# Shifted bias table, four-tile state products, later top-k steps and a last row by halves in a two-layer streaming encoder step

## The chip, the cores and the metric

The kernel runs on one core of a Trainium2 chip, written by hand for each engine: TensorE (PE, with its weight loads PEld), VectorE (DVE), ScalarE (ACT), GpSimd (POOL) and SyncE (SP), which issues most of the DMAs. The metric is the device time of one execution in microseconds (us). Three runs of the kernel before took 1894.93, 1895.78 and 1898.64 us; their median, 1895.78 us, is the time before.

## The reference

One inference step of a two-layer hybrid encoder over 640 tokens: 512 frames of a new stream (prompt) and 8 running streams of 16 frames (sample). All is fp32.

```python
def rmsnorm(x, g):
    xf = x.astype(jnp.float32)
    y = xf * lax.rsqrt(jnp.mean(xf * xf, axis=-1, keepdims=True) + EPS)
    return (y * g.astype(jnp.float32)).astype(x.dtype)
...
# layer 0, per query: score all visible keys with a small indexer, keep the top ones, attend to them
score = jnp.einsum('bqhs,bqh->bqs', jax.nn.relu(s), wi_b.astype(jnp.float32)) * IDX_SCALE
score = jnp.where(visible[None], score, -jnp.inf)
top_s, top_i = lax.top_k(score, top)
bias = bias_tab[rel_bucket(top_i - pos_b[None, :, None])]
logits = (jnp.einsum('bqgjd,bqkgd->bqgjk', q_b, k_sel).astype(jnp.float32) * ATTN_SCALE
          + jnp.moveaxis(bias, 2, -1))
probs = jax.nn.softmax(logits, axis=-1).astype(v_sel.dtype)
...
# layer 1: a Mamba-2 mixer: in-projection, causal conv of 4 taps, SiLU, chunked state recurrence
def step(s, inp):
    st, dec = inp
    return s * dec[..., None, None] + st, s
...
x = x + out.astype(x.dtype)
x = x + sqrelu_mlp(rmsnorm(x, norm_ffn[i]), mlp_w_up[i], mlp_w_down[i]).astype(x.dtype)
```

The outputs are the normalized x of both groups, and the new keys, values, indexer keys, conv rows and states. There are 16 heads of 64 with 4 key/value heads, 8 SSM groups of 4 heads, d_model 1024, d_ff 4096. The top of a query is 128 keys of 512 (prompt) or 132 of 528 (sample).

## The kernel before, in words

**Layout.** Activations lie transposed in SBUF: `xT` is 128 partitions x 8 chunks x 640 tokens. Every large product is split in three (high x high, low x high, high x low parts of fp32): for each of 8 chunks of the contraction, three weights by two halves of 320 tokens (`chunk_products`, line 206), so 48 matmuls a block of 128 output columns. A block's weights are loaded by SP into one of two slots (`load_slab`, L181), split by ACT (`split_hi`, L194: `WH`) and DVE (`split_lo`, L198: `WL`), and its product stands in two PSUM banks: 0 and 1, or 2 and 3, by the block's parity. A slot's load waits until the weights two blocks before have been split.

**What orders the work.** There is no scheduler: every engine has a program written out in order, and waits on semaphores. An instruction that waits holds up all that stands behind it on its engine.

**Stages, with their place in the time of the profile.**
1. 0 to 119 us: x is turned, block by block the indexer queries, indexer keys, keys and values are projected. The relative-position table (32 buckets x 16 heads) is expanded by a product with a one-hot matrix (L2328), copied by ACT (`tb_stage`), stored to DRAM (L2119) and read back skewed, 16 rows at a time, into `biasP` and `biasS` (L2127, L2137) by the same SP queue that loads the weights. The norm's scales are spread over the partitions by `norm_pe_spread` (L287).
2. 119 to 187 us: eight query blocks; between the halves of each, the cached indexer keys and the sample scores; DVE runs the 16 top-k rounds of the prompt.
3. 187 to 286 us: prompt attention in 64 units (2 key/value pairs x 4 query tiles x 8 heads; tile t has 128(t+1) keys). POOL adds mask and bias into `BM` (L2247 for the far keys, which share one bias `cfar`; L2249 for the near ones), PE multiplies (L2423), DVE adds and takes the maximum (`maxed`, L2964), ACT takes the exponent (L2697), PE turns (L2436) and weighs (L2450). Once in 8 units `spread_sums` (L2462) spreads the inverse sums, 8 products of 64 columns into bank 7, which ACT copies (L2714) before the next exponent. Between the units DVE makes the masks (`mask_step`) and runs the sample's top-k (`sample_top`: L2951, L2953, L2955), one step a unit.
4. 286 to 347 us: sample attention. 347 to 405 us: the attention's output blocks `B_O` to `B_O + 7`, added to x (L426).
5. 405 to 839 us: the MLP of layer 0, as pairs of 128 columns, with products by quarters (L1370, L1398). The rows of the last pairs are added to x by `add_row` (L1616).
6. 839 to 1446 us: the SSM. Eight groups of six blocks; during group g the products of group g-1 (u) finish. Within a group's first two blocks PE turns the old sample states (`pe_turn_prev`, L554, into banks 6 and 7), ACT copies them (`copy_prev`, L912), PE makes the states' new parts (`pe_sample_states`, L565, banks 4 and 5) and DVE adds them (`sample_states`, L719, 8 instructions). POOL multiplies the decays (`multiply_w`, L1047). The last group finishes beside the output blocks `B_OUT`.
7. 1446 to 1893 us: the MLP of layer 1 and the final norm: sums (L1811), the last chunk's squares (L1820), turned rows (L1799), scaled by ACT (L1839) and DVE (L1855), stored by SP (L1916).

## Time and profile before

| what | value |
|---|---|
| median of three runs | 1895.78 us |
| the profiled execution, its own time | 1895.32 us |
| its span | 1893.4 us |
| mean granted TensorE clock | 0.993 |
| PE, DVE, ACT, POOL busy | 98%, 67%, 42%, 16% |
| chain that ended last: PE | 86% |
| the same: DVE, issue, ACT, DMA | 4%, 4%, 3%, 1% |

The execution's own time is 1.9 us more than its span. The span runs from the first instruction to the last; what lies around it is start and the landing of the last stores. A busy share of PE is not PE at its peak, since the ends of matmuls are modelled. The chain is followed back from the last instruction, and the shares tell on which engine the time passed.

### The profile page before, as it was taken

How to read it: one execution, taken by the hardware profiler on the slowest of the kernel's cores; microseconds unless marked ns; L12 is line 12 of the kernel's file. 1: busy time of each engine (PE TensorE's matmuls, PEld its weight loads, DVE VectorE, ACT ScalarE, POOL GpSimd, SP SyncE). 2: the span in 40 equal slices, each digit the busy share in tenths (PEclk: the TensorE clock that was granted, in tenths of full speed). 3: DMA queues.
4: the chain of work that ended last, by engine and by line, in shares of the span. 5: the costliest groups of instructions: out<-in, count | busy, mean ns of one | idle time of the engine just before them, and what ended most of it. 6: DMA issues, size and time to landing. Idle time of an engine off the chain costs nothing.

```text
span 1893.4 us, 35381 instructions
## 1 busy us (share of the span) xinstructions
PE 1848.0 (98%) x13223; PEld 1737.0 (92%) x13223; DVE 1271.5 (67%) x2357; ACT 801.7 (42%) x1435; POOL 303.5 (16%) x356
## 2 busy tenths in 40 slices
PE   8899899999999999999999999999999999999998
PEld 7777566899999999999999999999899999999998
DVE  4388875447758586447787888888554775858653
ACT  4232674334334343334465544656333434434332
POOL 0001651110000000022333343332112000000001
PEclk9999999999999999999999999999999999999999
DMA  6732203331322223322433444335423132222321
GB/s 154 128 74 53 64 24 125 77 95 57 112 62 73 84 78 94 97 55 82 129 101 123 130 133 133 102 122 164 148 67 110 51 112 62 83 75 87 92 68 56
DMA packets 311571, 176.88 MB, mean 93 GB/s; under 512 B 39888, under 2 KB 305040, under 8 KB 310416
## 3 DMA queue, kind: packets, MB, share of 16 engines
q1 hardware_dynamic: 308752, 172.49, 32.3%
q10 hardware_dynamic: 2688, 2.62, 0.5%
q8 instruction: 86, 1.41, 0.3%
q14 instruction: 45, 0.37, 0.1%
HBM read 155.18 MB, written 19.72 MB: 92 GB/s over the span
## 4 chain that ended last, share of the span: by engine, by line
PE 86%; DVE 4%; issue 4%; ACT 3%; DMA 1%; SPq 1%; DVEq 0%; POOL 0%; ACTq 0%
PE psum L206 29%; PE psum L1370 28%; PE psum L1398 14%; PE psum L589 1%; PE psum L2423 1%; PE psum L2436 1%; PE psum L2515 1%; PE psum L2450 1%; PE psum L565 1%; DMA W<-attn_w_in 1%; PE psum L593 1%; PE psum L554 1%; PE psum L542 1%; DVE conv_out L708 1%; PE psum L2354 1%
## 5 line engine op out<-in xcount | busy, mean ns | idle before, releaser
L206 PE MATMUL psum<-b2H,WH 128*128 128x320 f32 x912 | 218.2, 321 | 1.2 <-DVE xT L1616 0.9
L206 PE MATMUL psum<-b2H,WL 128*128 128x320 f32 x912 | 208.6, 310 | 0.0
L206 PE MATMUL psum<-b2L,WH 128*128 128x320 f32 x912 | 208.4, 310 | 0.0
L1370 PE MATMUL psum<-b2H,HT 128*128 128x320 f32 x816 | 186.2, 309 | 1.1 <-DVE xT L426 1.1
L1370 PE MATMUL psum<-b2L,HT 128*128 128x320 f32 x816 | 186.0, 309 | 0.0
L194 ACT ACTIVATE WH<-W 128x1024 fp32r<-128x1024 f32 x90 | 95.0, 1055 | 201.9 <-PE psum L206 161.5
L198 DVE TENSOR_TENSOR WL<-W,WH 128x1024 fp32r<-128x1024 f32 x90 | 139.7, 1552 | 55.8 <-ACT WH L194 54.9
L1398 PE MATMUL psum<-HH,HT 128*128 128x320 f32 x544 | 167.4, 308 | 1.5 <-DVE HL L1487 1.5
L1398 PE MATMUL psum<-HL,HT 128*128 128x320 f32 x544 | 167.8, 308 | 0.0
L206 PEld LDWEIGHTS psum<-b2H,WH 128*128 128x128 f32 x912 | 150.0, 190 | 16.0 <-issue 12.6
L206 PEld LDWEIGHTS psum<-b2L,WH 128*128 128x128 f32 x912 | 153.4, 189 | 0.0
L1370 PE MATMUL psum<-b2H,LT 128*128 128x320 f32 x672 | 153.1, 309 | 0.0
L206 PEld LDWEIGHTS psum<-b2H,WL 128*128 128x128 f32 x912 | 153.1, 189 | 0.0
L1426 DVE SCALAR_TENSOR_TENSOR HF<-psum,RS 128x640 f32<-128x640 f32 (+1 forms) x70 | 53.1, 766 | 136.6 <-PE psum L1370 129.3
L1398 PE MATMUL psum<-HH,LT 128*128 128x320 f32 x448 | 138.0, 308 | 0.0
L1370 PEld LDWEIGHTS psum<-b2H,HT 128*128 128x128 f32 x816 | 136.3, 188 | 1.4 <-issue 1.4
L248 POOL COPY ACC<-SQ 128x640 f32<-128x640 f32 x4 | 4.3, 1072 | 825.8 <-ACT SQ L235 786.1
L1370 PEld LDWEIGHTS psum<-b2L,HT 128*128 128x128 f32 x816 | 136.3, 188 | 0.0
L206 PE MATMUL psum<-b1H,WH 128*128 128x320 f32 (+1 forms) x528 | 125.9, 320 | 6.6 <-DVE WL L198 5.2
L1431 ACT ACTIVATE HF<-HF 128x640 f32<-128x640 f32 (+1 forms) x70 | 48.4, 692 | 190.2 <-DVE HF L1426 190.2
L206 PE MATMUL psum<-b1H,WL 128*128 128x320 f32 (+1 forms) x528 | 121.6, 312 | 0.0
L206 PE MATMUL psum<-b1L,WH 128*128 128x320 f32 (+1 forms) x528 | 121.2, 311 | 0.0
(398 smaller groups left out, 4368.1 us busy)
## 6 DMA issues: line engine op xcount, KB each, us to landing
W<-ssm_w_in SPq DMA_DIRECT2D x98, 256.0 KB, 3.1
RW<-mlp_w_up SPq DMA_DIRECT2D x64, 256.0 KB, 3.0
RWx<-mlp_w_up SPq DMA_DIRECT2D x64, 256.0 KB, 3.0
RW<-mlp_w_down SPq DMA_DIRECT2D x64, 256.0 KB, 3.1
RWx<-mlp_w_down SPq DMA_DIRECT2D x64, 256.0 KB, 3.1
bc<-scratch_acs SPq DMA_DIRECT2D x8, 1280.0 KB, 7.5
W<-attn_w_in SPq DMA_DIRECT2D x32, 256.0 KB, 3.9
prev<-state_ssm SPq DMA_DIRECT2D x16, 512.0 KB, 5.3
```

The lines of the kernel that those rows point to most:

```text
L194: act.activation(WH[:, b.slot], W[:, b.slot], ACT.Copy).then_inc(w_hi, 1)
L198: dve.tensor_tensor(WL[:, b.slot], W[:, b.slot], WH[:, b.slot].bitcast(F32), ALU.subtract).then_inc(w_lo, 1)
L206: last = pe.matmul(psum[0:m, 2 * b.slot + h, 0:TH], w[:, b.slot, k, 0:m], r[:, k, h * TH:(h + 1) * TH], start=(n == 0 and i == 0), stop=(n ...
L542: last = pe.matmul(bank(4, 1024, 2)[:, 256 * t + P * p:256 * t + P * p + P], Btok[:, t * P:(t + 1) * P], xddt[:, p, t * P:(t + 1) * P], st ...
L554: last = pe.transpose(bank(6, 1024, 2)[:, b * P:(b + 1) * P], prev[:, p, b], ident)
L565: last = pe.matmul(bank(4 + k), xddt[r, p, SEQ:T], Bx[r, 4 * k:4 * k + 4].rearrange("p b n -> p (b n)"), start=True, stop=True)
L589: pe.matmul(bank(6, T, 2)[64 * h:64 * h + 64, t * P:(t + 1) * P], xdt[:, p, t * P + 64 * h:t * P + 64 * h + 64], Wm[:, 2 * p + h, t * P:(t ...
L593: pe.matmul(psum[:, 4, (t - 1) * P:t * P], ST[:, t - 1, p * P:(p + 1) * P], C2[:, t * P:(t + 1) * P], start=True, stop=True)
L1370: last = pe.matmul(psum[:, i // 2 * 2 + h, 0:TH], w[:, k], x, start=(kx == 0 and c == 0), stop=(kx == 7 and c == 2))
L1398: last = pe.matmul(down_bank(g, i), w[:, k], x[:, DNB[i], k], start=(k == 0 and c == 0), stop=(k == 3 and c == 2))
L1426: dve.scalar_tensor_tensor(t, src, 0.0, rs, ALU.max, ALU.mult).then_inc(h_rl, 1)
L1431: act.activation(t, t, ACT.Square).then_inc(h_sq, 1)
```

## The change

- **Table.** The one-hot row of the far bucket gets -1 everywhere, so that every bias is taken relative to the far one (softmax does not see a shift common to a head). `cfar` and its load go. POOL's far part becomes a copy of the mask, and only for the first four units after a change of tile.
- **Bias loads.** The 16 loads of `biasP` and `biasS` move from between the blocks 4, 5 and 6 into the first six query blocks on SP. The table's product and the turned vectors come ahead of `norm_pe_spread` and of two products of block 1 on PE.
- **Attention.** `sample_top` starts at unit 18 in place of 12, the sample's mask at 52 in place of 46. `spread_sums` alternates between the two halves of the columns.
- **Banks at two stage changes.** Block `B_O + 7` goes to banks 6 and 7, row 1 of pair 31 to banks 4 and 5, and the first products of the next stage wait for one block or row less.
- **SSM.** `pe_sample_states` is 4 products of 32 rows x 256 columns into banks 4 to 7, in place of 2 of 64 x 512 into 4 and 5; it now waits for `copy_prev` too. DVE's `sample_states` of the first half comes ahead of `split_lo`. ACT's SiLU of the second gate (`silu_second`) moves from a group's end to behind the first `copy_prev` of the next, and the second `copy_prev` comes ahead of `silu_rows`.
- **End.** The last row is multiplied, added and squared by halves of the tokens; the sums come between the halves. The last tile is scaled half by ACT and half by DVE, and its store is issued by ACT.

```diff
@@ shape_constants
+    onehot[half - 1] -= 1.0
@@ Block
+            self.out = 6 if c == B_O + 7 else 2 * self.slot
@@ pe_turn_prev, p == 1
+            pe.wait_ge(fss, 16 * u + 4)
@@ pe_sample_states
         pe.wait_ge(bxs, u + 1)
+        pe.wait_ge(pvc, 3 * u + p + 1)
...
-        for k in range(2):
-            r = slice(64 * k, 64 * k + 64)
-            last = pe.matmul(bank(4 + k), xddt[r, p, SEQ:T], Bx[r, 4 * k:4 * k + 4].rearrange("p b n -> p (b n)"),
+        for i in range(4):
+            r = slice(32 * i, 32 * i + 32)
+            last = pe.matmul(psum[:, 4 + i, 0:256], xddt[r, p, SEQ:T], Bx[r, 2 * i:2 * i + 2].rearrange("p b n -> p (b n)"),
                              start=True, stop=True)
@@ sample_states
-        for b in range(DB):
+        for b in (4, 5, 6, 7, 0, 1, 2, 3):
@@ ssm_group_dve
-        conv_evac(dve, g, 0)
+        conv_evac(dve, g, 0, (lambda: sample_states(dve, u, 0)) if L else None)
...
-        if L:
-            sample_states(dve, u, 0)
         conv_taps(dve, g, 0)
@@ ssm_group_act
+    def silu_second(act, u):
+        act.wait_ge(out_free, (Block(B_SSM + 5, 3 * u)).n + 1)
+        act.activation(sz[:, 1], sz[:, 1], ACT.Silu).then_inc(zs, 1)
...
         split_hi(act, b0(0), 4)
+        if L:
+            silu_second(act, u)
+            copy_prev(act, u, 1)
...
         silu_rows(act, g, 0)
-        if L:
-            copy_prev(act, u, 1)
...
-        act.wait_ge(out_free, (Block(B_SSM + 5, 3 * g)).n + 1)
-        act.activation(sz[:, 1], sz[:, 1], ACT.Silu).then_inc(zs, 1)
@@ rows_pe
+    def row_bank(g, r):
+        return 4 if (g, r) == (31, 1) else 2 * r
...
-                    pe.wait_ge(out_free, last_block(layer, i // 2) + 1)
+                    pe.wait_ge(out_free, B_O + 6 if (g, i) == (0, 0) else last_block(layer, i // 2) + 1)
...
+                last_row_pe(pe)
+                return
...
+    def last_row_pe(pe):
...
+        for h in range(2):
+            for i in (2, 3):
+                n, b = n0 + i, ((0, 3), (4, 5))[i % 2][h]
+                for k in range(4):
+                    for c, (w, x) in enumerate(((HT[h_tile(n)], HH), (HT[h_tile(n)], HL), (LT[l_tile(n)], HH))):
+                        last = pe.matmul(psum[:, 2 + h, 0:TH], w[:, k], x[:, b, k],
+                                         start=(i == 2 and k == 0 and c == 0), stop=(i == 3 and k == 3 and c == 2))
+            last.then_inc(sw_mm, 1)
+            if h == 0:
+                final_sums(pe)
@@ mlp_dve, the last row of layer 1
+            for h in range(2):
+                dve.wait_ge(sw_mm, op0(63) + 3 + h)
+                dve.wait_ge(sw_cb, 56)
+                dve.tensor_tensor(x_half(7, h), psum[:, 2 + h, 0:TH], x_half(7, h), ALU.add).then_inc(sw_rx, 1)
@@ final_pe
-        pe.wait_ge(sq_ready, 40)
-        for t in range(NT):
-            last = pe.matmul(psum[:, 0, t:t + 1], SQ[:, 1, t * P:(t + 1) * P], ones[:], start=False, stop=(t == NT - 1))
-        last.then_inc(x_turn, 1)
+        pe.wait_ge(sw_rx, 17)
+        final_squares(pe, 1).then_inc(x_turn, 1)
@@ tail_pe
-        pe.wait_ge(sw_rx, 8)
+        pe.wait_ge(sw_rx, 6)
         multiply(pe, Block(B_DT), b2H, b2L, ready=(gx_lo, 16), order=ORD)
@@ tail_dve, last group
         add_to_x(dve, Block(B_OUT), 0)
+        sample_states(dve, u, 0)
         split_lo(dve, Block(B_OUT + 2))
-        sample_states(dve, u, 0)
         add_to_x(dve, Block(B_OUT + 1), 1)
+        sample_states(dve, u, 1)
         split_lo(dve, Block(B_OUT + 3))
-        sample_states(dve, u, 1)
@@ sync, query blocks
+                if b < 6:
+                    for n in range((0, 2, 4, 7, 10, 13)[b], (2, 4, 7, 10, 13, 16)[b]):
+                        load_bias_p(DS * n) if n < 8 else load_bias_s(n - 8)
@@ gpsimd, units
-                if far:
-                    pool.tensor_tensor(BM[:, u % 4, 0:far], maskP[:, OFF[t]:OFF[t] + far],
-                                       cfar[:, h:h + 1].broadcast_to([P, far]), ALU.add)
+                if far and u % 8 < 4 and TILES[u // 8 - 1][1] != t:
+                    pool.tensor_copy(BM[:, u % 4, 0:far], maskP[:, OFF[t]:OFF[t] + far])
@@ tensor, first blocks
             first_products(1, 4)
+            first_products(0, 7)
+            pe.wait_ge(c_in, 112)
             pe.wait_ge(x_ready, 8)
-            norm_pe_spread(pe, 0)
-            first_products(0, 7)
-            first_products(1, 5)
-            pe.wait_ge(c_in, 112)
             pe.matmul(psum[0:NH, 7, 0:512], rb_stage[:], oh_stage[:, 0:512], start=True, stop=True)
...
+            norm_pe_spread(pe, 0)
+            first_products(1, 5)
@@ spread_sums
-                for gj in range(8):
-                    gp, j = gj // 4, gj % 4
-                    last = pe.matmul(psum[64 * gp:64 * gp + 64, 7, j * P:(j + 1) * P],
-                                     rinv[:, w % 2, 2 * j + gp:2 * j + gp + 1].broadcast_to([P, 64]), ident, start=True, stop=True)
+                for j in range(4):
+                    for gp in range(2):
...
@@ vector, units
-                if 12 <= u < 46:
-                    sample_top(u - 12)
-                if 46 <= u < 53:
+                if 18 <= u < 52:
+                    sample_top(u - 18)
+                if 52 <= u < 59:
```

**SP, from the table's constants to the first query blocks.** `W` is the weight slot of `load_slab`, `scratch_bias` the table in DRAM. Before:

```order
L181 DMA W<-attn_w_in 128x4x128 x2
L2119 DMA scratch_bias<-tb_stage 256x1x656
L181 DMA W<-attn_w_in 128x4x72 x2
L2127 DMA biasP<-scratch_bias 16x16x256 x4
L181 DMA W<-attn_w_in 128x4x128 x2
L2127 DMA biasP<-scratch_bias 16x16x256 x4
L181 DMA W<-attn_w_in 128x4x128 x2
L2137 DMA biasS<-scratch_bias 16x2x528 x8
L2140 DMA cfar<-rel_bias 128x16
L181 DMA W<-attn_w_in 128x4x128 x4
L2145 DMA kiT<-kiT 64x640
L2146 DMA scratch_wi<-wiT 8x128
```

With the change:

```order
L183 DMA W<-attn_w_in 128x4x72 x2
L2173 DMA scratch_bias<-tb_stage 256x1x656
L183 DMA W<-attn_w_in 128x4x128 x6
L2178 DMA kiT<-kiT 64x640
L2179 DMA scratch_wi<-wiT 8x128
L183 DMA W<-attn_w_in 128x4x128 x2
L2184 DMA wcol<-scratch_wi 16x8x1 x8
L2203 DMA KI<-cache_idx_k 128x4x64 x4
L183 DMA W<-attn_w_in 128x8x64 x8
L2203 DMA KI<-cache_idx_k 128x4x64 x2
L2191 DMA biasP<-scratch_bias 16x16x256 x2
L183 DMA W<-attn_w_in 128x8x64 x2
```

The loads of `biasP` no longer stand between those of `W`; the first two come behind `KI` and eight loads of `W`, in the first query block.

**ACT, from the last group's exponent on.** `Wm` is the decays, `prevT` the turned sample states, `sz` the gate. Before:

```order
L957 ACTIVATE Wm<-Wm 128x2560
L1012 ACT_TABLE_LOAD
L1012 ACTIVATE sz<-sz 128x640
L912 ACTIVATE prevT<-psum 128x8x128
L194 ACTIVATE WH<-W 128x1024
L912 ACTIVATE prevT<-psum 128x8x128
```

With the change:

```order
L959 ACTIVATE Wm<-Wm 128x2560
L914 ACTIVATE prevT<-psum 128x8x128
L196 ACTIVATE WH<-W 128x1024
L963 ACT_TABLE_LOAD
L963 ACTIVATE sz<-sz 128x640
L914 ACTIVATE prevT<-psum 128x8x128
```

The gate's table load and SiLU have gone from between the exponent and the first copy of `prevT` to behind the first split.

**DVE, in a group's first block.** `raw` is the block taken from PSUM, `prev` the sample states, `WL` the low part of the next weights. Before:

```order
L689 TENSOR_TENSOR raw<-psum,RS 128x192
L690 TENSOR_TENSOR raw<-psum,RS 128x8x16
L198 TENSOR_TENSOR WL<-W,WH 128x1024
L719 SCALAR_TENSOR_TENSOR prev<-prev,EXp,psum 128x128 x8
L711 TENSOR_SCALAR conv_out<-raw,cw 128x664
L708 SCALAR_TENSOR_TENSOR conv_out<-raw,cw,conv_out 128x664 x3
```

With the change:

```order
L692 TENSOR_TENSOR raw<-psum,RS 128x192
L693 TENSOR_TENSOR raw<-psum,RS 128x8x16
L722 SCALAR_TENSOR_TENSOR prev<-prev,EXp,psum 128x128 x8
L200 TENSOR_TENSOR WL<-W,WH 128x1024
L714 TENSOR_SCALAR conv_out<-raw,cw 128x664
L711 SCALAR_TENSOR_TENSOR conv_out<-raw,cw,conv_out 128x664 x3
```

The eight steps on `prev` have moved ahead of the split of the next weights.

## Rows read from the trace of the kernel before

**Rows 1.** page, busy time, share of the span and instructions of each engine

```profile
PE 1848.0 (98%) x13223; PEld 1737.0 (92%) x13223; DVE 1271.5 (67%) x2357; ACT 801.7 (42%) x1435; POOL 303.5 (16%) x356
```

**Rows 2.** chain that ended last, 25 to 125 us; start, length, what

```profile
54.29 13.97 DMA W<-attn_w_in
```

**Rows 3.** who waited for whom, whole run; total us, times, longest us

```profile
PE psum L206 <- DVE WL L198: 5.2, 2, 4.6
...
PE psum L1370 <- DVE xT L426: 1.1, 1, 1.1
...
PE psum L206 <- DVE xT L1616: 0.9, 1, 0.9
...
PE psum L565 <- DVE prev L719: 1.0, 1, 1.0
```

**Rows 4.** busy time by stretch; PE, PEld, DVE, ACT, POOL, then PE clock, DMA share, GB/s

```profile
60.00:66.00 6.00, 5.58 (x22) 5.58 (x23) 1.92 (x3) 0.00 (x0) 0.00 (x0) 0.54 1.19 176
66.00:70.00 4.00, 4.00 (x28) 3.73 (x26) 0.62 (x1) 1.06 (x1) 0.00 (x0) 1.00 1.05 208
206.20:216.60 10.40, 8.24 (x72) 5.04 (x73) 9.99 (x28) 4.85 (x16) 7.88 (x12) 1.00 0.46 136
276.10:284.00 7.90, 6.82 (x66) 4.68 (x66) 3.70 (x20) 5.63 (x25) 3.24 (x10) 1.00 0.42 138
```

**Rows 5.** timeline of VectorE and TensorE, 27 to 29 us

```profile
27.57 0.88 DVE L239 SCALAR_TENSOR_TENSOR b1L<-xT,vcol,b1H 128x640 fp32r<-128x640 f32 x1
27.80 1.35 PE L287 MATMUL psum<-cst,rs 128*128 128x128 f32 x10 [1.01 <-DVE rs L282]
```

**Rows 6.** DMA issues, 0 to 130 us; KB each, median us to landing

```profile
W<-attn_w_in SPq DMA_DIRECT2D x28, 256.0 KB, 4.3
...
biasP<-scratch_bias SPq DMA_DIRECT2D x8, 256.0 KB, 11.7
```

**Rows 7.** timeline of the SP queue, 105 to 350 us

```profile
137.02 1.00 SPq L181 DMA_DIRECT2D W<-attn_w_in  x2
```

**Rows 8.** chain that ended last, 120 to 187 us

```profile
165.59 3.71 PE psum L206 x24
```

**Rows 9.** chain that ended last, 187 to 292 us

```profile
228.51 1.18 PE psum L2462 x13
229.97 0.07 PE psum L2462
...
234.31 1.02 PE psum L2450 x16
...
288.86 0.86 PE psum L2515 x2
```

**Rows 10.** chain that ended last, 1136 to 1196 us

```profile
1148.52 1.06 PE psum L565 x4
...
1162.46 1.00 PE psum L576 x16
```

**Rows 11.** timelines of ACT, DVE and POOL, 1143 to 1154.2 us

```profile
1144.06 2.34 ACT L957 ACTIVATE Wm<-Wm 128x2560 f32<-128x2560 f32 x1
...
1148.76 0.49 DVE L688 TENSOR_TENSOR raw<-psum,RS 128x320 f32<-128x320 f32 x1 [2.18 <-PE psum L206]
...
1150.35 3.08 DVE L198 TENSOR_TENSOR WL<-W,WH 128x1024 fp32r<-128x1024 f32 x1 [0.64 <-ACT WH L194]
...
1146.64 5.71 POOL L1047 TENSOR_TENSOR Wm<-Wm,cbm 128x2560 f32<-128x2560 f32 x1 [14.24 <-ACT Wm L957]
```

**Rows 12.** timelines of ACT and PE, 1325 to 1338 us

```profile
1325.82 2.34 ACT L957 ACTIVATE Wm<-Wm 128x2560 f32<-128x2560 f32 x1
...
1327.06 1.13 PE L565 MATMUL psum<-Bx,xddt 64*128 64x512 f32 x4 [0.47 <-DVE ST L799]
```

**Rows 13.** chain that ended last, 1860 us to the end

```profile
1879.65 1.01 PE psum L1811 x10
...
1881.38 1.25 PE psum L1820 x10
```

More of the change, by code:

```diff
@@ L205, in chunk_products @@
             for h in range(2):
-                last = pe.matmul(psum[0:m, 2 * b.slot + h, 0:TH], w[:, b.slot, k, 0:m],
+                last = pe.matmul(psum[0:m, b.out + h, 0:TH], w[:, b.slot, k, 0:m],
                                  r[:, k, h * TH:(h + 1) * TH],
@@ L425, in add_to_x @@
         xd = xT[:, d] if isinstance(d, int) else xT[:, bass.ds(d, 1)].rearrange("p o t -> p (o t)")
-        dve.tensor_tensor(halves(xd), out_all(b.slot), halves(xd), ALU.add).then_inc(out_free, 1)
+        dve.tensor_tensor(halves(xd), psum[:, b.out:b.out + 2, 0:TH], halves(xd), ALU.add).then_inc(out_free, 1)
     s2 = [S0]
@@ L1764, in mlp_act @@
                 down_act(act, g, end)
-        next_act(act, layer, 7)
+        if layer:
+            act.wait_ge(acc_done, 38)
+            for h in range(2):
+                act.wait_ge(sw_rx, 16 + h)
+                act.activation(SQ[:, 1, h * TH:(h + 1) * TH], x_half(7, h), ACT.Square).then_inc(sq_ready, 1)
+        else:
+            next_act(act, layer, 7)
         if layer == 0:
@@ L1781, in mlp_dve @@
                 down_dve(dve, g, end)
-        add_row(dve, 32 * layer + 31, 1)
+        if layer:
+            for h in range(2):
+                dve.wait_ge(sw_mm, op0(63) + 3 + h)
+                dve.wait_ge(sw_cb, 56)
+                dve.tensor_tensor(x_half(7, h), psum[:, 2 + h, 0:TH], x_half(7, h), ALU.add).then_inc(sw_rx, 1)
+            dve.wait_ge(sw_rx, 17)
+        else:
+            add_row(dve, 31, 1)
         next_dve(dve, layer, 7)
@@ L1811, in final_pe, with final_squares @@
             pe.matmul(psum[:, 0, t:t + 1], ACC[:, t * P:(t + 1) * P], ones[:], start=(t == 0), stop=False)
+    def final_squares(pe, half):
+        pe.wait_ge(sq_ready, 40 + half)
+        for t in ((0, 1), (2, 3, 4))[half]:
+            last = pe.matmul(psum[:, 0, t:t + 1], SQ[:, 1, t * P:(t + 1) * P], ones[:], start=False, stop=(t == NT - 1))
+        return last
+    def final_pe(pe):
+        final_squares(pe, 0)
         pe.wait_ge(newton, 16 + 7)
@@ L1814, in final_pe @@
             y_turn(pe, t, ORD[6])
-        pe.wait_ge(sw_rx, 16)
-        for i in range(4):
+        pe.wait_ge(sw_rx, 17)
+        final_squares(pe, 1).then_inc(x_turn, 1)
+        for i in range(KC - 1):
             y_turn(pe, 2, ORD[i])
-        pe.wait_ge(sq_ready, 40)
-        for t in range(NT):
-            last = pe.matmul(psum[:, 0, t:t + 1], SQ[:, 1, t * P:(t + 1) * P], ones[:], start=False, stop=(t == NT - 1))
-        last.then_inc(x_turn, 1)
         for i in range(4, KC - 1):
@@ L1913, in tail_sp @@
             load_pair(sp, g)
-        for t in range(NT):
+        for t in range(4):
             sp.wait_ge((rs_ready, newton)[t % 2], (8 + 2, 16 + 14)[t % 2] + t // 2)
-            sp.dma_start(O["y_prompt"].rearrange("b s d -> (b s) d")[P * t:P * t + P, :] if t < 4 else
-                         O["y_sample"].rearrange("b i d -> (b i) d"), y_tok[:, t]).then_inc(store, 16)
+            sp.dma_start(O["y_prompt"].rearrange("b s d -> (b s) d")[P * t:P * t + P, :], y_tok[:, t]).then_inc(store, 16)
         for s, n in ((pv_st[0], SG), (pv_st[1], SG), (sp_st, SG), (y_st, SG - 1), (store, 8 + NT)):
@@ L2152, in _, with load_bias_p, load_bias_s @@
                                  allow_slow_non_contiguous=True).then_inc(wi_col, 16)
+            bt = S["bias"]
+            def load_bias_p(p0):
+                sp.dma_start(biasP[p0:p0 + DS], skew(bt, -REL0 - P - p0, [[NREL - 1, DS], [DS * NREL, NH], [1, 256]])
+                             ).then_inc(bias_in, 16)
+            def load_bias_s(gj):
+                sp.dma_start(biasS[DS * gj:DS * gj + DS],
+                             skew(bt, gj * DS * NREL + DS - 1,
+                                  [[NREL - 1, DS], [8 * DS * NREL, 2], [1, KEYS_S]])).then_inc(bias_in, 16)
             def load_ki(b):
@@ L2459, in spread_sums @@
                 wait(pe, rbc, w)
-                for gj in range(8):
-                    gp, j = gj // 4, gj % 4
-                    last = pe.matmul(psum[64 * gp:64 * gp + 64, 7, j * P:(j + 1) * P],
-                                     rinv[:, w % 2, 2 * j + gp:2 * j + gp + 1].broadcast_to([P, 64]), ident, start=True, stop=True)
+                for j in range(4):
+                    for gp in range(2):
+                        last = pe.matmul(psum[64 * gp:64 * gp + 64, 7, j * P:(j + 1) * P],
+                                         rinv[:, w % 2, 2 * j + gp:2 * j + gp + 1].broadcast_to([P, 64]), ident,
+                                         start=True, stop=True)
                 last.then_inc(rsp, 1)
@@ L2635, in _ @@
             act.sem_inc(sq_ready, 3)
+            split_hi(act, Block(2))
             norm_act_copy(act, 0)
-            for b in range(2, 9):
+            act.wait_ge(v_rdy, 4)
+            act.activation(tb_stage[:, 0:512], psum[0:NH, 7, 0:512], ACT.Copy)
+            act.activation(tb_stage[:, 512:NREL], psum[0:NH, 4, 256:256 + NREL - 512], ACT.Copy).then_inc(v_rdy, 1)
+            for b in range(3, 9):
                 split_hi(act, Block(b))
-                if b == 2:
-                    act.wait_ge(v_rdy, 4)
-                    act.activation(tb_stage[:, 0:512], psum[0:NH, 7, 0:512], ACT.Copy)
-                    act.activation(tb_stage[:, 512:NREL], psum[0:NH, 4, 256:256 + NREL - 512], ACT.Copy).then_inc(v_rdy, 1)
             def index_relu(n):
```

64 lines of the change are left out of this document (33 added, 31 removed).

## The prediction

> **What bounds the kernel.** I read the busy times first. TensorE is busy 98% of the span [rows 1], VectorE 67%, ScalarE 42%, GpSimd 16%. A change can therefore shorten the time in two ways only: it removes a wait of TensorE, or it removes work of TensorE. Work saved on the others counts only where TensorE waits for them. The span is 1893.4 us; the profiled execution's own time is 1895.32 us, which lies 0.46 us under the median of the runs. The sum is made on the former, and 0.46 is added at the end.
>
> Next I read who waited for whom on TensorE, which gives four waits that the diff touches [rows 3]: 5.2 us in two for the low weights `WL` (the longest 4.6 us), 1.1 and 0.9 us at the two stage changes, 1.0 us for the sample states of the last group. Then I read the stretches around them: clock and load [rows 4], the chain of the attention [rows 9], of an SSM group [rows 10] and of the end [rows 13].
>
> **Start, 0 to 119 us.** The reader sees in the chain that a DMA of `W` took 13.97 us from 54.29 on [rows 2], where such a load of 256 KB takes 4.3 us in the middle case [rows 6]. The loads of `biasP`, of which each has the same 256 KB and a median of 11.7 us [rows 6], stood ahead of it in the same queue. This slab's split came too late, and TensorE stood still for 4.6 us. With the change no bias load stands between these slabs, so both waits go: -5.2 us. The standing still had a second price. From 60 to 66 us TensorE had a granted clock of 0.54, its lower level of 1.2 GHz, and 22 matmuls took 5.58 us; right behind, at a clock of 1.00 (2.4 GHz), 28 took 4.00, 0.143 each [rows 4]. At that pace the 22 take 3.14, so -2.4 us more.
>
> Against it: the one-hot product now comes ahead of the norm's spread product and takes a place among the first products, and the spread's successor waits for the low parts of x. VectorE finishes the last of these at 27.57 + 0.88 = 28.45 [rows 5]. TensorE waited 1.01 us until 27.80 before, so it was free at 26.79, and now it stands until 28.45, 1.66 us: +0.65. The one-hot constants must be there earlier; I take 0, with an upper end of +0.5. Start in all: -5.2 - 2.4 + 0.65 = -6.95.
>
> **Query blocks, 119 to 187 us.** The bias loads now stand here, two or three a block, on the same SP queue. A slab issued at 137.02 [rows 7] belongs to the products that TensorE begins at 165.59 [rows 8], 28 us later, about 26 after the splits. Even a landing of 13.97, as seen behind such loads, leaves 12 us. So I price the move at 0; without this lead it would cost what it cost at the start. The attention's first biases are wanted only after 187 us.
>
> **Attention, 187 to 286 us.** `spread_sums` stands in the chain with 13 records and 1.18 us at 228.51 and its last at 229.97, to 230.04: 1.53 us from first to last [rows 9]. ScalarE must copy the result before its next exponent. The turned products of L2450, which go by pairs of column halves, put 16 records into 1.02 us [rows 9], one per 0.064. L2462 before ran all four of one half of the columns and then all four of the other. Alternating halves should bring it to about 1.02, 0.5 less, of which I take 0.45. It happens 8 times, in 7 of them with the exponents waiting behind: -3.2. Bounds: 0, if the two halves do not lie beside each other, and -4.
>
> The top-k of the samples goes six steps later. From 206.2 to 216.6 us VectorE is busy 9.99 of 10.40 us and TensorE 8.24; from 276.1 to 284, where six steps now land, VectorE is busy 3.70 of 7.90 [rows 4]. The six steps of about 0.6 us are taken out of the full stretch, and about a third of that reaches TensorE: -1.3, between -2.3 (the whole of TensorE's 2.16 idle there) and +0.5 (they delay the last units' maxima). The masks then come six units later, and the loads behind them still land before the sample products at 288.86. GpSimd's lighter `BM` I count at 0: it was 7.88 of 10.40 busy in the full stretch, not the last to arrive. Attention: -4.5.
>
> **Stage changes.** The waits of 1.1 and 0.9 us [rows 3] are for the last block or row to leave its banks. With spare banks they go; with the refill 0.1 more: -2.1. The next that could be late is the last chunk of x, wanted only behind seven other chunks, which is hidden.
>
> **SSM.** Two products of 64 rows x 512 columns are 4 records in 1.06 us [rows 10]. One product of this kind with 512 columns, L2515, is 2 records in 0.86 [rows 9]. So the two lie beside each other, with some 0.2 fixed, else they would take 1.72. Four of 32 rows x 256 columns side by side would take 0.43 + 0.2 = 0.63, a gain of 0.43. Bounds, for 32-row tiles no row shows: best 0.43 (-0.63); pairwise only, 1.06 (0); one after the other 1.92 (+0.86). I take side by side, since 16 records of L576, tiles by columns, fit into 1.00 [rows 10], and price 7 groups x 2 x -0.43 = -6.0.
>
> The Trainium skill, "TensorE: Matmul & The Clock Gate", Part 3 on packing small matmuls, gives four 32-row tiles of 512 columns a measured speedup of 3.07. By it 1.72 would become about 0.56, an estimate, and the gain would be 0.50 in place of 0.43, -7.0 in all. No run here shows it yet.
>
> The product now waits for ScalarE's copy of the old states too. In a steady group the exponent ends at 1144.06 + 2.34 = 1146.40 [rows 11]; the copy behind it takes about 1.0, so to 1147.4, and TensorE wants it at 1148.52 [rows 10]: 1.1 us to spare, 0. Queued behind a late copy would be all of TensorE. The second turn now waits for four of VectorE's steps on the states. They stand ahead of the split, behind the copies of `raw`, about 1149.7 to 1150.8, and are wanted some 2 us later: 0. This holds if these steps are not slowed beside GpSimd's product of the decays, which runs from 1146.64 for 5.71 [rows 11]. Beside it `raw`, with one input from SBUF and one from PSUM, took 0.49, while the split, both inputs in SBUF, took 3.08 [rows 11]. The steps on `prev` take PSUM and SBUF, so I count them undisturbed.
>
> The Trainium skill, "SBUF — State Buffer", on who interferes with whom, says the same of a VectorE instruction with two SBUF inputs against a reading GpSimd one, and that whichever starts first blocks the other. By this the split, which now starts about 1 us later, would wait less; the sum does not change, since its result is wanted far later.
>
> In the last group ScalarE has its exponent until 1325.82 + 2.34 = 1328.16 [rows 12]; before, TensorE began its product at 1327.06, since it didn't wait for the copy. Now it can start at 1328.16 + 1.01 = 1329.17 at the earliest: +2.1. Then the later wait of 1.0 for the states [rows 3] goes and two products are cheaper by 0.86: +0.2 net.
>
> **End.** The sums L1811 (1.01) and squares L1820 (1.25) stand behind the last row [rows 13]. The sums now run between the halves, and two of five squares are done early, against smaller instructions on the way: -0.4. The stores behind are bound by the transfers, so who issues them moves nothing. Bounds -1.5 and +0.5.
>
> **Sum.** -6.95 - 4.5 - 2.1 - 6.0 + 0.2 - 0.4 = -19.75. 1895.32 - 19.75 = 1875.6, and with 0.46: 1876.
>
> **Rivals.**
> - *32-row tiles do not lie beside each other four at a time.* For it: no row has them. Against: the 64-row ones do. The 14 products gain nothing: 1876 + 6 = 1882. In full series they cost 14 x 0.86 in place of -6.0, +18: 1894, no change.
> - *Another half-clock spell.* The last group's wait of 2.6 us (0.47 + 2.1) or the 1.66 us of the start could bring what the 4.6 us brought. Price 2.4 to 3.5 us: 1879.5. Against: the rows show one only behind 4.6 us.
> - *The attention passes the wait on.* ScalarE's exponents wait on VectorE's maxima, so shorter spreading is given back: 0 in place of -4.5, 1880.5.
> - *The states' steps are blocked beside GpSimd* as the split is (3.08 against about 1.2): then the second turn comes about 0.7 late in 7 groups: +4.9, 1881.
> - *The slower one: the bias loads starve the query blocks.* Here the queue has 16 more loads within 60 us. It decides once a slab lands more than 26 us after its issue, against 13.97 seen. If slabs came 5 us late in five of the blocks, 25 us would come on top: 1901. Against: the share of the DMA engines is under half in most stretches of the middle part (0.46, 0.42), though over 1 at 60 to 70 us [rows 4].
>
> **How the numbers follow.** 0.66 for the forecast (its own range 1871 to 1881, from the bounds of the top-k, spreading and tile terms), 0.12 for tiles without a gain, of which 0.02 is full series; 0.10 for a new spell, 0.05 for the attention, 0.04 for blocked steps, 0.03 for starved query blocks. The range goes from 1869, where tiles, spreading and the end all reach their lower ends (-2.8, -0.8, -1.1 and -1.0 from the top-k, -5.7 together, and 1 for small waits), to 1885. About 0.2%, 3.8 us, is what a measurement can tell from no change: faster, under 1892, has all but the starved blocks and full series: 0.95; same 0.02; slower 0.03.
>
> **What would show it.** Start: TensorE without a wait for `WL` over 1 us and a granted clock of 1.00 from 60 to 66 us; if a wait stays, the term falls. Query blocks: no wait for `WL` from 119 to 187. Attention: L2462's successor with 16 records in about 1.0. SSM: four tiles with starts within 0.1 and about 0.63 in all; a wait for `prevT` in steady groups would be against me. Last group: TensorE waits about 2.6 us for `prevT` and none for `prev`. I am wrong outside the range if the tiles run serially or a slab of the query blocks comes late.

## The result, and the profile after

| | us |
|---|---|
| before, median of 4 runs | 1895.36 |
| changed, median of 4 runs (1876.36 to 1880.72) | 1878.08 |
| ratio, 95% interval | 0.9909, [0.9893, 0.9925] |
| profiled execution: own time, span | 1876.36, 1874.6 |

The change makes the kernel 17.3 us faster by the medians, 19.0 us by the two profiled executions (1895.32 against 1876.36). Forecast was 1876, range 1869 to 1885. The busy times after, as those of [rows 1]:

```profile
PE 1834.3 (98%) x13290; PEld 1731.4 (92%) x13290; DVE 1259.0 (67%) x2359; ACT 802.1 (43%) x1436; POOL 290.1 (15%) x336
```

The last store lands 0.48 us ahead of the span's end in both executions (1892.97 and 1874.09), so what an execution takes beyond its span, 1.8 to 1.9 us, is not that landing.

TensorE is still the bound. Its work is 13.7 us less. Since both kernels issue almost the same products in the same order, the best view of where the time went is the start of the same product in both traces. Each number is the growth, over one stage, of the start after minus the start before. A clock stretch is a time in which TensorE's granted clock was 0.50, its lower level of 1.2 GHz:

| stage | forecast | measured | of which |
|---|---|---|---|
| start and query blocks, to the first L2501 (193.29 before, 188.24 after) | -6.95 | -5.05 | the two waits for `WL` are gone, a clock stretch has moved to 29 to 36 us |
| attention, to 288.15 / 275.65 | -4.5 | -7.45 | -2.7 is a clock stretch (193 to 199 us) that did not come |
| two stage changes, to 846.71 / 831.69 | -2.1 | -2.5 | |
| begin of the SSM, to 898.14 / 883.85 | 0 | +0.7 | -3.05 and +3.8, below |
| seven SSM groups, to 1280.83 / 1259.53 | -6.0 | -7.0 | |
| last group, to 1342.04 / 1322.51 | +0.2 | +1.8 | a clock stretch behind the wait |
| end, to TensorE's last (1886.24 / 1866.87) | -0.4 | +0.2 | |
| stores behind it | 0 | +0.5 | from the first issue to the last landing 8.34 us, before 7.86 |

The waits of TensorE, whole run, that answer to [rows 3] (columns: who waited for whom, total us, times, longest):

```profile
PE psum L208 <- DVE b1L L241: 2.6, 3, 1.8
PE psum L568 <- ACT prevT L914: 2.6, 1, 2.6
PE psum L536 <- ACT Btok L998: 2.0, 1, 2.0
```

All four waits of [rows 3] are gone. Three others stand there. The first and the second were forecast (1.66 and 2.6 us; they are 1.8 and 2.56); the third, 2.0 us for `Btok`, was not. The stretches around them, as in [rows 4] (PE, PEld, DVE, ACT, POOL, then PE clock, DMA share, GB/s):

```profile
28.00:36.00 8.00, 7.81 (x28) 5.38 (x29) 1.99 (x6) 2.08 (x4) 0.00 (x0) 0.58 0.18 37
50.00:60.00 10.00, 10.00 (x71) 9.75 (x69) 2.73 (x3) 1.69 (x2) 0.00 (x0) 1.00 0.27 74
191.00:199.00 8.00, 6.31 (x61) 3.85 (x59) 6.80 (x25) 5.41 (x19) 5.96 (x9) 1.00 0.47 159
871.00:878.00 7.00, 5.18 (x38) 4.91 (x36) 6.78 (x8) 1.57 (x5) 4.12 (x7) 1.00 0.48 156
878.00:884.00 6.00, 5.78 (x31) 5.81 (x32) 4.26 (x3) 5.89 (x8) 4.09 (x4) 0.72 0.15 38
...
191.00:199.00 8.00, 7.04 (x35) 4.37 (x33) 4.92 (x19) 3.86 (x17) 3.28 (x5) 0.57 0.13 37
871.00:878.00 7.00, 7.00 (x28) 6.70 (x28) 4.44 (x5) 5.16 (x8) 0.35 (x2) 0.51 0.34 92
878.00:884.00 6.00, 6.00 (x43) 6.00 (x42) 5.12 (x9) 1.06 (x1) 1.33 (x2) 1.00 0.65 176
```

The first five rows are of the changed kernel, the last three of the one before. From 50 to 60 us, where the kernel before stood still for 4.6 us, TensorE is now busy all the time at 1.00. But from 28 to 36 us it had a granted clock of 0.58, where it ran 28 matmuls in 7.81 us. The stretch at 0.50 of the kernel before at 191 to 199 us is absent (1.00), and the one at 871 to 878 has its counterpart at 878 to 884 (0.72). Inside the kernel these stretches last 3.41 or 6.83 us in all fourteen profiles. At half the clock a TensorE that is busy throughout does 1.7 or 3.4 us less work in them; where it also waits in them, the starts of equal products show somewhat less (1.5, 2.7 us).

The products of the states and the spread sums, as in [rows 9] and [rows 10] (chain that ended last):

```profile
218.70 1.05 PE psum L2513 x16
...
1130.20 0.64 PE psum L568 x8
...
1138.94 0.64 PE psum L568 x8
```

`spread_sums` has 16 records in 1.05, 0.48 less than before; the four row tiles take 0.64, forecast 0.63, where the two took 1.06.

The last group, as in [rows 11] and [rows 12] (timelines of ACT and PE):

```profile
1304.52 2.34 ACT L959 ACTIVATE Wm<-Wm 128x2560 f32<-128x2560 f32 x1
1306.77 1.00 ACT L914 ACTIVATE prevT<-psum 128x1024 f32<-128x1024 f32 x1
...
1307.87 0.71 PE L568 MATMUL psum<-Bx,xddt 32*128 32x256 f32 x8 [2.56 <-ACT prevT L914]
...
1309.66 0.73 PE L208 MATMUL psum<-b2H,WH 128*128 128x320 f32 x2
1310.19 0.73 PE L208 MATMUL psum<-b2L,WH 128*128 128x320 f32 x2
```

The exponent ends at 1306.86, the copy at 1307.77, and L568 starts 0.10 later behind 2.56 us of standing still. That is as forecast. The pairs of matmuls right behind it take 0.53 from start to start (1309.66 to 1310.19) in place of 0.29: the lower clock. It costs 1.5 us more, which was only among the rivals.

### The profile page after: what moved, and what is told of

It reads as the page before. It is cut to its first block, busy times and chain, and to the rows that moved or that the text cites. A ratio compares the mean times of both kernels' runs of the same rounds, so it can differ in the third digit from the quotient of the medians.

```text
span 1874.6 us, 35518 instructions
## 1 busy us (share of the span) xinstructions
PE 1834.3 (98%) x13290; PEld 1731.4 (92%) x13290; DVE 1259.0 (67%) x2359; ACT 802.1 (43%) x1436; POOL 290.1 (15%) x336
## 4 chain that ended last, share of the span: by engine, by line
PE 88%; DVE 4%; issue 3%; ACT 3%; DMA 0%; DVEq 0%; POOL 0%; SPq 0%; ACTq 0%
PE psum L208 32%; PE psum L1380 27%; PE psum L1426 14%; PE psum L592 1%; PE psum L2474 1%; PE psum L2567 1%; PE psum L2487 1%; PE psum L556 1%; PE psum L596 1%; PE psum L2501 1%; PE psum L543 1%; PE psum L2405 1%; PE psum L568 1%; PE psum L2591 1%; DVE conv_out L711 0%
## 5 line engine op out<-in xcount | busy, mean ns | idle before, releaser
L200 DVE TENSOR_TENSOR WL<-W,WH 128x1024 fp32r<-128x1024 f32 x90 | 126.7, 1408 | 27.2 <-ACT WH L196 27.0
```

The lines of the kernel that those rows point to most:

```text
L200: dve.tensor_tensor(WL[:, b.slot], W[:, b.slot], WH[:, b.slot].bitcast(F32), ALU.subtract).then_inc(w_lo, 1)
```

## The experiments

Each kernel was compared with the changed one by the starts of equal products in the profiles. "Theory" and "rival" below are what was expected before each run. Medians have 4 or 5 runs (the very last one a single run). The runs of one kernel differ by up to about 7 us, in part by clock stretches that fall here or there, so effects of 1 to 4 us are read from the traces.

**The state products again as two of 64 rows.**

```diff
-        for i in range(4):
-            r = slice(32 * i, 32 * i + 32)
-            last = pe.matmul(psum[:, 4 + i, 0:256], xddt[r, p, SEQ:T], Bx[r, 2 * i:2 * i + 2]...
+        for k in range(2):
+            r = slice(64 * k, 64 * k + 64)
+            last = pe.matmul(bank(4 + k), xddt[r, p, SEQ:T], Bx[r, 4 * k:4 * k + 4]...
...
```

VectorE's `sample_states` reads banks 4 and 5 accordingly.

> The changed kernel, but the new parts of the sample states again as 2 products of 64 rows x 512 columns in place of 4 of 32 x 256; waits and orders stay as changed. Theory (four row tiles lie beside each other, and this is the whole gain of the SSM stage): L568 goes from 0.65 us a time to about 1.06, and the stage gets 0.41 x 16 = 6.6 us longer, about 1884.5 in all. Rival (the stage's gain comes from the moved waits and the order on ScalarE and VectorE, not from the product): the product's time is hidden by a wait behind it, and the stage stays within 1.5 us of the changed kernel's.

Measured: 1882.83 us, ratio to before 0.9935 [0.9916, 0.9954]. In the chain of its trace:

```profile
1132.86 1.06 PE psum L568 x4
...
1142.03 1.06 PE psum L568 x4
```

1.06 each, and each of the 14 in the steady groups moves all that follows by 0.39 to 0.42 us: +5.5 at the last group. The product is the gain of the SSM stage; the rival falls. In all its last product of TensorE is 4.3 us later: the last group loses less, since its clock stretch at 1309 us did not come (-1.5).

**`spread_sums` by one half of the columns and then the other.**

```diff
-                for j in range(4):
-                    for gp in range(2):
+                for gp in range(2):
+                    for j in range(4):
```

> The changed kernel, but spread_sums writes all four products of the one column half and then all four of the other. Theory: the 16 records take about 1.5 us in place of 1.0, and each of the seven times that exponents wait behind costs 0.48: +3.4 us in the attention, about 1881. Rival (the wait is passed on): the records take longer but the stage's length changes by under 1 us.

Measured: 1880.44 us. The chain has it as the kernel before:

```profile
218.15 1.18 PE psum L2513 x13
```

ScalarE's copies behind it come later by 0.47 to 0.48 us each of eight times: from 1.02 us ahead of the changed kernel at the first to 2.30 behind at the last, with 1.49 ahead of all. So 3.8 us, and nothing is passed on. Forecast was 0.45 seven times; it is 0.48 eight times, none is hidden. The profiled execution is only 2.0 us longer than the changed kernel's, since its stretch at 31 us was the short one (1.5 us less); its other stretches nearly cancel.

**Top-k from unit 12 again.**

```diff
-                if 18 <= u < 52:
-                    sample_top(u - 18)
+                if 12 <= u < 46:
+                    sample_top(u - 12)
```

and the sample's mask from unit 46.

> The changed kernel, but the samples' top-k starts at unit 12 and their mask at unit 46 again. Theory: the 1.7 us that TensorE gained in units 12 to 17 go again, and nothing is gained at the end: +1.7 us, about 1879.7. Rival (the gain there came from GpSimd's lighter bias or from elsewhere): 0. Also watched: whether the stretch at half the clock at the attention's begin, which one profile of the kernel before showed (191.8 to 198.6 us) and that of the changed one did not, appears; all instructions up to there are those of the changed kernel, so that a difference would be chance.

Measured: 1880.61 us. The waits of TensorE, 195 to 215 us, of this kernel and then of the changed one:

```profile
PE psum L2513 <- DVE rinv L3022: 1.5, 1, 1.5
...
PE psum L2513 <- DVE rinv L3022: 0.2, 1, 0.2
```

The third call of `spread_sums` waits 1.5 us for VectorE's inverse sums, 0.2 with the later top-k (the kernel before had this wait too, 1.53 us at 215.04): the start of its first product is 1.43 us later, and no difference arises from there to the end of the attention but a clock stretch at 207 to 211 us (0.56). Forecast -1.3, measured -1.4, but the place is one wait, not a third of the load taken off VectorE: that the sizes meet is luck. At the attention's begin no stretch at half the clock came. In five of the fourteen profiles of this case it did (before, bias loads back, table first, sums behind both halves, the four mends once), in the others not.

**Bias loads between the slabs again.**

```diff
-            for b in range(5, 8):
-                load_slab(sp, Block(b), slab_g1(b))
+            for p0 in range(0, 64, DS):
+                load_bias_p(p0)
+            load_slab(sp, Block(5), slab_g1(5))
...
```

The other loads follow between blocks 6 and 7, and those in the query blocks go.

> The changed kernel, but the 16 bias loads stand between the weight slabs of blocks 4 to 7 on SP again. Theory: TensorE waits some 5 us for WL near 55 to 62 us and then runs at the lower clock level for 3 to 7 us: +7 to +8 us, about 1885. Rival A (the 4.6 us wait came from the table's store and read-back, which both stand early here too, so the slabs are late only as far as TensorE is early): +3 to 5. Rival B (the loads cost nothing here since the spell at half the clock at 29 to 36 us has slowed TensorE by then): under 2.

Measured: 1886.77 us, ratio 0.9952 [0.9935, 0.997]. Waits of TensorE 60 to 130 us, and its stretches:

```profile
PE psum L208 <- DVE WL L200: 4.4, 2, 3.6
...
62.00:69.00 7.00, 4.91 (x34) 4.65 (x32) 0.00 (x0) 0.88 (x1) 0.00 (x0) 1.00 1.17 180
69.00:75.00 6.00, 4.51 (x22) 4.51 (x23) 2.40 (x3) 1.24 (x2) 0.30 (x1) 0.72 1.03 216
```

The wait is 4.4 us in all, followed by a clock of 0.72 from 69 to 75 us. From 0.50 us ahead of the changed kernel at 58 us it goes to 5.74 behind at the first L2396 (79.03), 6.2 us: 4.5 of waiting and refill and 1.7 of clock. That lies between the theory (7 to 8) and rival A; rival B falls. The rest of the 9.9 us in this profile are clock stretches at 192 to 200 and 281 to 286 us.

**Table ahead of the last first product.**

```diff
             first_products(1, 4)
-            first_products(0, 7)
             pe.wait_ge(c_in, 112)
...
+            first_products(0, 7)
             norm_pe_spread(pe, 0)
```

> The changed kernel, with the table's product and the turned vectors moved ahead of the last first product (0, 7) of block 0, so that they fill the 1.8 us in which TensorE waited for the low part of x's last chunk. Theory (the wait of 1.8 us, standing still, is what brought the stretch at half the clock from 29 to 36 us): the wait goes or is under 0.3 us, the clock stays at 1.00 until 40 us, and block 1 ends 1.8 + 3.4 = 5.2 us earlier; at 73 us (the first L2393) the kernel is 4.5 to 5.2 us ahead of the changed one. Rival A (a stretch at half the clock comes near there whatever stands still, since it follows other things): only the 1.8 us are gained. Rival B (the gained time is lost to the slabs from SP, which are late instead): under 1 us at 73 us.

Measured: 1872.33 us, ratio 0.9875 [0.9855, 0.9895]. Timeline and stretch of TensorE:

```profile
26.51 1.03 PE L2376 MATMUL psum<-oh_stage,rb_stage 32*16 32x512 f32 x2
...
28.39 0.53 PE L208 MATMUL psum<-b1H,WH 128*128 128x320 f32 x2
...
28.00:36.00 8.00, 8.00 (x55) 7.65 (x56) 4.66 (x8) 3.63 (x6) 0.00 (x0) 1.00 0.35 58
```

The products of the table fill the gap, the wait shrinks from 1.8 to under 0.5 us, the clock from 28 to 36 us is 1.00 and 55 matmuls run there in place of 28. At 73 us the kernel is 4.73 us ahead. The theory holds: with the 1.8 us of standing still the lower clock went as well. The edit also moves the table's products, which ran right behind the wait. That they rather than the wait brought the lower clock is unlikely, since in two of the ten profiles with the wait (tiles, the changed kernel's second) the stretch began ahead of them.

**The first copy of `prevT` ahead of the last exponent.**

```diff
         exponents(act, g, between)
+        if last:
+            copy_prev(act, g, 0)
         exp_w(act, g)
...
-        copy_prev(act, u, 0)
```

> The changed kernel, with ScalarE's first copy of prevT ahead of the exponent in the last group (in the changed kernel behind it). Theory: TensorE's wait of 2.56 us before L568 at 1305.3 shrinks to the 0.5 us that it had for ST before: -2.1 us, and where the half-clock stretch at 1309 to 1313 goes with it another -1.7. Rival (the decays that GpSimd multiplies are late instead, since the exponent ends 1 us later): a new wait of about 1 us at the product that reads Wm, net -1 us.

Measured: 1873.92 us, ratio 0.9893 [0.9875, 0.9911].

```profile
1304.11 0.71 PE L568 MATMUL psum<-Bx,xddt 32*128 32x256 f32 x8 [0.46 <-DVE ST L803]
```

The wait is 0.46 us and for `ST` again, -2.1 us; 0.4 comes back as a wait for `WL` and refill behind it, and the clock stretch is absent, -1.5: -3.2 in all. Nothing waits for the later decays. The 1.5 are not surely the mend's: four of the ten profiles that keep the wait have no stretch there either.

**`Btok` ahead of `silu_rows` in the first group.**

```diff
+        if g_is_first(g):
+            copy_b(act, g)
         silu_rows(act, g, 3)
-        act.wait_ge(tB, g + 1)
...
```

`copy_b` is the wait for `tB` and the copy into `Btok`.

> The changed kernel, with ScalarE's copy Btok ahead of the last silu_rows in the first group only. Theory: TensorE's wait of 2.04 us at L536 (878.2 us), which the kernel before did not have because a half-clock stretch at 871 to 878 had made TensorE late there, goes: -2.0 us, and no half-clock stretch at 879 to 883. Rival (the next in line, xs behind VectorE's convolution, is as late): the wait stays over 1 us with another name.

Measured: 1874.54 us. TensorE does not wait at L536. But a half-clock stretch at 858 to 863 us lay ahead of it. A stretch ahead makes TensorE later and hides the wait. How much is hidden shows in two other kernels, `spread_sums` by halves and the copy ahead of the exponent, which have a stretch of the same 3.41 us there and the old order. Their waits, 840 to 900 us:

```profile
PE psum L536 <- ACT Btok L998: 0.5, 1, 0.5
...
PE psum L536 <- ACT Btok L998: 0.5, 1, 0.5
```

0.5 with the old order behind such a stretch, 0 with the new one, 2.0 to 2.1 in the five profiles with the old order and no stretch ahead (the changed kernel twice; tiles, bias loads and banks back). Behind a stretch of 6.83 us TensorE does not wait with the old order either (top-k back, table first, sums behind both halves). So the mend is worth nothing there and about 0.6 us behind a short stretch; the 2 us without one were not seen.

**Sums behind both halves.**

```diff
-            if h == 0:
-                final_sums(pe)
 ...
     def final_pe(pe):
+        final_sums(pe)
         final_squares(pe, 0)
```

> The changed kernel, with the sums L1853 behind both halves of the last row again in place of between them. Theory (between the halves their 1.03 us stand on the path, while behind the last half they lie beside VectorE's add and ScalarE's square, 0.97 us): -0.6 to -0.9 us from the last product's begin to the first store. Rival (VectorE's add of the first half and the squares then come too late): 0.

Measured: 1876.67 us. Chain at its end, as [rows 13]:

```profile
1854.46 7.04 PE psum L1402 x48
1861.50 1.01 PE psum L1851 x10
1862.51 0.45 PE psum L1856 x4
```

The 48 products run through in 7.04, and the sums stand where VectorE and ScalarE do the last half. From 1.35 us behind the changed kernel at 1852 us, ahead of the last row, it comes to 0.55 behind at the end: -0.8, as expected. The four mends together show the same 0.8, twice.

**Banks at the stage changes back.**

```diff
-            self.out = 6 if c == B_O + 7 else 2 * self.slot
+            self.out = 2 * self.slot
...
```

> The changed kernel, but block B_O + 7 in banks 2 and 3 again, row 1 of pair 31 in banks 2 and 3, and the first products of the next stage waiting for the last block or row. Theory: TensorE waits 1.1 and 0.9 us there again, with the refill some +1.3 and +1.2, +2.5 us in all. Rival (the gain at the changes came from the chunk's copies, which other parts of the change bring earlier): under 1 us.

Measured: 1881.4 us, ratio 0.993 [0.9915, 0.9945]. Waits, whole run:

```profile
PE psum L1380 <- DVE xT L427: 1.1, 1, 1.1
...
PE psum L208 <- DVE xT L1644: 0.9, 1, 0.9
```

1.1 and 0.9 again, and from the second product behind each on the starts are 1.36 and 1.18 us later: 2.5 in all.

**The changed kernel once more, and the four mends together, twice.**

> The changed kernel itself, beside the others on the same chip, 1878 us. Its profile is the second one of the same program. Theory (half-clock stretches behind a wait of TensorE of 1.8 us or more come each time, the others by chance): stretches at 29 to 36 and 1309 to 1313 us again, the one at 879 to 883 only if none lies in the 20 us ahead of it, others may come at 187 to 199, 333 to 341 and 855 to 867. Rival (a program has its stretches at fixed places): the same four places as in the first profile, and no others.

> All four mends together: the table ahead of the last first product, the first copy of prevT ahead of the last group's exponent, Btok ahead of silu_rows in the first group, the sums behind both halves of the last row. Theory (each removes a wait of its own, and the gains add): -4.5 at the start, -2.0 at L568 and up to -1.7 with the clock stretch behind it, -2.0 at L536 where no half-clock stretch lies ahead of it, -1.0 at the end; some -9 against the changed kernel run beside it, with up to 3 us either way by where half-clock stretches fall, about 1868. Rival (the stretches at half the clock only move to other places once one is avoided, so that their sum stays): -5 to -6.

> The four mends together once more, for one profile: in both earlier profiles with Btok ahead of silu_rows a half-clock stretch at 854 to 863 lay ahead and hid the place. Theory: where no such stretch lies between 850 and 870 us, TensorE does not wait at L536 and no stretch at half the clock follows at 875 to 885; the time is 1868 to 1871. Rival: a wait of over 1 us stands there with another name. If the stretch lies ahead again, the profile cannot tell.

Measured side by side on one chip: changed kernel 1878.2 us, ratio 0.9913 [0.99, 0.9927]; four mends 1870.46 us, ratio 0.9871 [0.9856, 0.9886]; once more 1869.1. The mends bring 7.7 us by the medians and 6.2 and 7.3 by the two profiled executions, against -9 expected and -5 to -6 of the rival: between the two.

In the first profile the start gives 3.0 (TensorE was 1.6 us late at 24 us already, ahead of the mend's place; the mend itself gives 4.6), the last group 3.2 and the end 0.8. Stretches at 332 to 336 and 854 to 862 us, which the first profile of the changed kernel did not have, cost 4.6, and 3.8 came back at `Btok`. These 3.8 are not the mend's: three kernels with the old order and the same 6.83 us stretch ahead get the same 3.8. The second profile again has a stretch ahead (855 to 859 us), so by what was expected of it, it cannot tell what the `Btok` mend is worth without one. It has no wait at L536.

The second profile of the changed kernel has its stretches where the first had them (29 to 37, 879 to 884, 1309 to 1314 us) and its starts within 0.7 us. But the two profiles of the four mends, one program too, have them at different places (332 and 854 us; 183, 268, 333 and 855 us), so the rival falls. The theory holds for the 1.8 us wait, behind which one came in all ten profiles; behind the longer wait of 2.56 us one came in only six of ten.

## Why the prediction was right, point by point

- **Start: right in the removed part, mis-sized by the clock.** -8.1 us were gained between the 90th and the 300th product of the start, where 7.6 was forecast. The step that failed is "+0.65" for the wait for x's last low part: the wait was 1.8 for 1.66, but a lower clock came behind it. It cost 4.2 in place of 0.65. It stood among the rivals with 0.10, "against" it that the rows show such a spell only behind 4.6 us. The rows did, but the trace of the kernel before did not: it has two more stretches of 6.83 us, at 191.78 us behind a wait of 0.87 and at 871.04 us with no wait over 0.3 us in the 10 us ahead.
- **Query blocks: right.** No wait for `WL` from 100 to 182 us; the biggest there is 1.3 us for `Rs`, as before.
- **Attention: right in its terms** by the undoing runs (3.8 for 3.2, 1.4 for 1.3), the second by luck in its size. The further 2.7 us are a clock stretch that one profile had and the other not. These make 7.9 of the measured 7.45, so nothing is left over for GpSimd's lighter mask and bias, counted at 0; no run puts that work back.
- **Stage changes: right**, 2.5 in the comparison and by the undoing run, for 2.1.
- **SSM: right.** 0.64 for 0.63; -5.7 of the -7.0 are the products (0.41 x 14), another 1.0 are four small waits for `Btok` in the later groups, which the changed kernel no longer has.
- **What was left out:** at the begin of the SSM the kernel before had a stretch at half the clock, and this kept TensorE behind ScalarE's `Btok`, as a stretch of that length does in three later kernels. Without it TensorE comes earlier, stands 2.0 us and has its lower clock then. The 3.05 us saved there go again, with 3.8 for the wait and its clock.
- **Last group: wait right, clock missed.** 2.56 us for 2.6; with the clock +1.8 in place of +0.2.
- **End: wrong sign.** "The sums now run between the halves", in the term of -0.4, read their 1.01 us in the chain [rows 13] as time that could be saved. Before they lay beside VectorE's add and ScalarE's square and cost next to nothing. The timeline of the kernel before, 1877 to 1894 us, has them so; the first squares' product starts behind the square:

```profile
1879.49 1.17 PE L1811 MATMUL psum<-ones,ACC 128*128 128x1 f32 x10
1879.69 0.82 DVE L1616 TENSOR_TENSOR xT<-psum,xT 128x640 f32<-128x640 f32 x1 [6.92 <-PE psum L1370]
1880.55 0.74 ACT L235 ACTIVATE SQ<-xT 128x640 f32<-128x640 f32 x1 [7.59 <-DVE xT L1616]
1881.34 1.27 PE L1820 MATMUL psum<-ones,SQ 128*128 128x1 f32 x10
```

Between the halves the sums are on the path. The undoing run gains 0.8. Another 0.5 came from the stores, forecast 0; why they took longer stays open.

In sum -19.75 was forecast, -18.96 is the difference of the profiled executions and -17.3 that of the medians. By the table, +1.9 at the start, +0.7 at the SSM's begin, +1.6 in the last group and +1.1 at the end and in the stores were met by -2.95 in the attention, -0.4 at the stage changes and -1.0 in the SSM groups. That the sum came out within 1 us of the forecast is partly luck: these cancel, and most of them are clock stretches, whose places differ from profile to profile.

The Trainium skill's "TensorE: Matmul & The Clock Gate", Part 3, on packed tiles, led, by its speedup of 3.07, to an estimate of 0.56 us for the row tiles; the trace has 0.64, so the sum by a fixed part read from rows, 0.63, was nearer. The Trainium skill, "SBUF — State Buffer", on who interferes with whom, states that a VectorE instruction with two SBUF inputs contends with a GpSimd instruction that reads SBUF, and that one with a single SBUF input, outside VectorE's two-port modes, does not. The trace agrees. VectorE's timeline in the last group, GpSimd's product of the decays running from 1306.94 to 1312.59:

```profile
1308.65 2.16 DVE L722 SCALAR_TENSOR_TENSOR prev<-prev,EXp,psum 128x128 f32<-128x128 f32 x8 [1.15 <-PE psum L568]
1310.72 2.95 DVE L200 TENSOR_TENSOR WL<-W,WH 128x1024 fp32r<-128x1024 f32 x1
...
1319.00 2.15 DVE L722 SCALAR_TENSOR_TENSOR prev<-prev,EXp,psum 128x128 f32<-128x128 f32 x8
1321.06 1.22 DVE L200 TENSOR_TENSOR WL<-W,WH 128x1024 fp32r<-128x1024 f32 x1
```

The steps on `prev`, from PSUM and SBUF, take 2.16 us beside it and 2.15 without it; the split, with both inputs in SBUF, 2.95 and 1.22.

## What to carry to other kernels

A wait of TensorE has two prices: the standing still, and the lower clock that may follow it; filling a wait of 1.8 us was worth 4.7 here. When a change makes TensorE earlier or adds a wait, look for short independent products that can stand in the gap, and for work that lies in another engine's queue ahead of what TensorE needs (an exponent of 2.34 us ahead of a copy of 1.0). And before work is moved off the end, look whether it lay beside something: there it was free.

## What the runs showed of the hardware

Stretches at the lower clock level (0.50 in the records) last 3.41 or 6.83 us inside the kernels and cost a busy TensorE half of that. Where they came, by place and by TensorE's wait just ahead, in the fourteen profiles:

| place, and the wait of TensorE ahead | profiles that have it | with a stretch |
|---|---|---|
| start, 1.8 us for x's last low part | 10 | 10 |
| the same place, wait filled | 3 | 0 |
| `Btok` at the SSM's begin, 2.0 to 2.1 us | 5 | 5 |
| last group, 2.56 us for `prevT` | 10 | 6 |
| the same place, 0.46 us for `ST` (the four mends twice, the copy first) | 3 | 0 |
| attention's begin, 0.87 and 0.96 us | 14 | 5 |
| end of the sample attention, 0.4 to 1.0 us | 14 | 8 |
| 854 to 867 us (871 before), none over 0.3 us in the 10 us ahead | 14 | 9 |

A stretch can begin while the wait still lasts: at 58.66 us in the kernel before, in a wait that ends at 60.42. What decides whether one comes the runs don't show. A part of the scatter of the runs, 1876.4 to 1880.7 us of one program, is of this kind: its four runs had mean clocks of 0.995, 0.994, 0.992 and 0.993 at 1876.36, 1878.0, 1880.72 and 1878.15 us.

Four products of 32 rows x 256 columns on different row groups take 0.64 us in all, two of 64 rows x 512 columns 1.06 us. Products of 64 columns that alternate between the column halves start 0.109 us apart in pairs; four of one half and then four of the other overlap only where the halves meet: 1.58 against 1.09 us from the first start to the last end (`spread_sums` in the undoing run and in the changed kernel).
